# Two-layer transformer block on one Trainium2 core: the mixed stage's projections in three passes of fp32r parts

## The chip, the cores and the metric

The program runs on one core of a Trainium2 chip. The time is the device time of one execution in microseconds, here the median of 3 runs. TensorE multiplies, VectorE, ScalarE and GpSimd do the elementwise work, SyncE issues the DMAs that bring the weights. Each engine runs its own instructions in program order and waits on semaphores.

## The reference

Two blocks follow each other on 256 tokens of width 1024, each with two layers. The change is in the first block only. Per layer it computes, cut to what matters:

```
h = rms_norm(x, norm1_g[l]) * (1.0 + sc1) + sh1
proj = h @ w_in[l]                       # 1024 -> 5648 columns
da_q, da_k, da_v, dn_q, dn_k, dn_v, dn_z, dn_b, dn_a, gates = jnp.split(proj, ...)
y_a = diff_attention(da_q, da_k, da_v, lam, ...)          # 4 heads, rope, two softmaxes each
y_b = gated_deltanet(dn_q, dn_k, dn_v, dn_z, dn_b, dn_a, dn_conv[l], ...)  # conv, chunked scan
g_a, g_b = jnp.split(jax.nn.sigmoid(gates), 2, axis=-1)
merged = g_a * (y_a @ w_branch_a[l]) + g_b * (y_b @ w_branch_b[l])
x = x + gt1 * (merged @ w_out[l])
h = rms_norm(x, norm2_g[l]) * (1.0 + sc2) + sh2
x = x + gt2 * (jnp.square(jax.nn.relu(h @ w_mlp1[l])) @ w_mlp2[l])
```

All of it is float32. The second block (windowed and latent attention, 16 experts) is not touched.

## The kernel before

**Weights.** All weights of the first block pass through a ring of 5 slots in SBUF, 2 MB each (128 partitions x 4096 floats). A list, `order`, gives the sequence of the loads; each load waits until the last reader of the block that was in its slot is done. ada blocks are the weights of the modulation vectors (step r reads one each, `ada_row`), win blocks those of the projections, gate blocks those of z and the gates.

**Layer.** For each of the two layers: the norm and its transpose into hT (fp32, 8 chunks of 128 x 256); the dense stage lin3, which makes attention's q, k and v in 12 groups; the mixed stage; branch_b and merged_out; the MLP. lin3, the branch of attention, merged_out and the MLP multiply in three passes of fp32r: a number is cut into a high part (ScalarE casts it to fp32r) and a low part (VectorE subtracts the high part from the number), and the product is high x high, low x high and high x low. An fp32r matmul has one record in the trace, an fp32 matmul two.

**Mixed stage.** It interleaves attention, the short convolutions, the delta rule and the remaining projections. Its sequence is one table, `mix_order()` (line 169), that every engine walks; each engine has a function for the steps in which it takes part. The step f with n from 0 to 11 is one block of 128 columns of the delta rule's q, k and v, with n from 13 to 32 one of z and the gates: 8 fp32 matmuls that read the weights in the ring and hT, in two or four pieces (`f_parts`, line 206). f 33 to 36 are the branch of attention in three passes. f 12, 37 and 38 only free banks or read results. The other steps that the prediction speaks of:

- a_prep, a_scale, a_rope, a_sum, a_turn: attention's q and k get norm and rope, on VectorE, and are transposed. s_core, e_soft, m_top, k_comb, t_prob, c_prob, v_val, o_val: scores, softmax, combination, values. a_hn, d_hn: the norms of the heads.
- d_conv, d_silu, d_tok: the convolutions, their silu, and the transposes back. d_gate, d_gcum, d_l2, d_kqT, d_decay, d_LT: gates, cumulative sums and decays up to the triangular matrices.
- d_X, d_B, d_U: the triangular inverse by doubling, on TensorE in 64x64 matmuls, with VectorE and ScalarE taking turns. d_uw: u and w. d_S, d_gl, d_ws, d_out: the scan over four chunks in two directions.
- r: one block of a modulation's weights. b_hi, b_lo: the parts of the branch's weights.
- rates (line 775): the 32 small matmuls for beta and the decay, between lin3 and the mixed stage.

Of the kernel before, what the change touches and what calls it, by code (L numbers as in the profile page):

```python
# [10 lines left out]
ALU = mybir.AluOpType  # L11
# [157 lines left out]
def mix_order():  # L169
# [3 lines left out]
        ("f", 0, 0), ("a_prep",), ("a_scale",), ("f", 0, 1), ("a_rope", 0), ("f", 1, 0), ("f", 1, 1), ("f", 2, 0),  # L173
        ("f", 2, 1), ("f", 3, 0), ("f", 3, 1), ("f", 4, 0), ("d_conv", 0), ("a_rope", 1), ("a_rope", 2),
        ("d_conv", 1), ("f", 4, 1), ("f", 5, 0), ("a_rope", 3), ("d_conv", 2), ("d_conv", 3), ("f", 5, 1),
        ("a_sum",), ("f", 6, 0), ("f", 6, 1), ("f", 7, 0), ("f", 7, 1), ("r", 0), ("a_turn", 0), ("a_turn", 2),
        ("a_turn", 1), ("a_turn", 3), ("d_silu", 0), ("s_core", 0), ("e_soft", 0, 0), ("e_soft", 0, 1), ("f", 8, 0),
        ("s_core", 1), ("m_top", 0, 0), ("d_tok", 0), ("e_soft", 1, 0), ("m_top", 0, 1), ("m_top", 1, 0),
        ("f", 8, 1), ("e_soft", 1, 1), ("m_top", 1, 1), ("d_conv", 4), ("f", 9, 0), ("r", 1), ("f", 9, 1),
        ("f", 10, 0), ("k_comb", 0), ("f", 10, 1), ("f", 11, 0), ("f", 11, 1), ("d_conv", 5), ("k_comb", 1),  # L180
        ("s_core", 2), ("f", 12, 0), ("e_soft", 2, 0), ("t_prob", 0), ("t_prob", 1), ("c_prob", 0), ("m_top", 2, 0),
        ("d_conv", 6), ("m_top", 2, 1), ("d_conv", 7), ("c_prob", 1), ("r", 2), ("e_soft", 2, 1), ("d_silu", 1),
# [10 lines left out]
        ("f", 27, 3), ("d_X",), ("d_B", 1), ("d_U", 1), ("d_B", 2), ("d_U", 2), ("d_B", 3), ("d_U", 3), ("d_B", 4),  # L193
        ("r", 7), ("d_U", 4), ("d_B", 5), ("r", 8), ("d_U", 5), ("d_uw", 0), ("d_uw", 1), ("d_S", 0, 0),
# [58 lines left out]
def program(nc, a, c1off, c2off, out):  # L253
    ctx = ExitStack()
    with ctx:
# [132 lines left out]
        for l in range(2):  # L388
            for i in range(4 if l == 0 else 0):
                ada(0, 0, i)  # L390
            for j in range(3):
                if l and j < 2:
                    for i in (2 * j, 2 * j + 1):
                        ada(1, 1, i)
                cols(("win", l, j), a["w_in"][l], 512 * j, 512)
            for step, *key in mix_order():
# [7 lines left out]
                if step == "f" and n == 13:  # L404
                    cols(("gate", l, 0), a["w_in"][l], 3072, 512)
# [2564 lines left out]
```

## Time and profile before

| what | us |
|---|---|
| median of 3 runs | 2265.42 (2264.52 to 2266.91) |
| the profiled execution's span, first to last instruction | 2264.9 |
| TensorE busy | 1930.7 (85%) |
| VectorE busy | 908.8 (40%) |
| ScalarE busy | 631.8 (28%) |
| DMA, over the span | 272 GB/s |

The profile is one execution. Its own time, start and end of the program included, is not listed apart; the runs' median lies 0.5 us over the span. The first block is the first half of the span: layer 0's mixed stage from 77.7 to 306.6 us, layer 1's from 585.5 to 815. Busy times of an engine are to be read against the stretch they stand in, and an idle engine matters only where another waits for it.

### The profile page before, as it was taken

How to read it: one execution, taken by the hardware profiler on the slowest of the kernel's cores; microseconds unless marked ns; L12 is line 12 of the kernel's file. 1: busy time of each engine (PE TensorE's matmuls, PEld its weight loads, DVE VectorE, ACT ScalarE, POOL GpSimd, SP SyncE). 2: the span in 40 equal slices, each digit the busy share in tenths (PEclk: the TensorE clock that was granted, in tenths of full speed). 3: DMA queues.
4: the chain of work that ended last, by engine and by line, in shares of the span. 5: the costliest groups of instructions: out<-in, count | busy, mean ns of one | idle time of the engine just before them, and what ended most of it. 6: DMA issues, size and time to landing. Idle time of an engine off the chain costs nothing.

```text
span 2264.9 us, 31221 instructions
## 1 busy us (share of the span) xinstructions
PE 1930.7 (85%) x12944; PEld 1292.3 (57%) x12944; DVE 908.8 (40%) x1518; ACT 631.8 (28%) x1090; POOL 43.2 (2%) x46
## 2 busy tenths in 40 slices
PE   6999999999999999999999766666798996666666
PEld 3878888987878889987755311211276552122111
DVE  2665575645665576645754100000058520000001
ACT  3243335544243235534451100000044310000001
POOL 0001000000001000000000000000000000000000
PEclk9999999999999999999999988888899998887878
DMA  9554248556523244554438999999972689999997
GB/s 337 227 192 187 77 184 299 187 186 237 208 75 150 85 177 151 185 189 113 175 141 330 429 426 426 428 427 427 425 236 112 273 337 427 428 426 426 428 427 307
DMA packets 117302, 617.50 MB, mean 273 GB/s; under 512 B 18304, under 2 KB 21290, under 8 KB 83370
## 3 DMA queue, kind: packets, MB, share of 16 engines
q1 hardware_dynamic: 116586, 613.85, 68.3%
q8 instruction: 103, 1.69, 0.3%
q10 hardware_dynamic: 576, 1.66, 0.2%
q14 instruction: 37, 0.30, 0.0%
HBM read 614.44 MB, written 1.05 MB: 272 GB/s over the span
## 4 chain that ended last, share of the span: by engine, by line
PE 60%; DMA 27%; DVE 7%; ACT 3%; issue 1%; SPq 0%; POOL 0%; DVEq 0%; ACTq 0%
PE pb L640 58%; DMA ring<-in_w_up_dram 17%; DMA ar<-in_w_up_dram 4%; DMA hT<-in_w_up_dram 4%; PE pb L643 3%; DVE ar L1574 2%; DVE ar L1566 2%; ACT ar L2339 1%; DMA ring<-in_w_down_dram 1%; DVE ar L1578 1%; DMA ring<-in_ada_w_dram 1%; ACT ar L2343 1%; DVE small L1582 1%; DVE ar L1570 0%; ACT hT L2339 0%
## 5 line engine op out<-in xcount | busy, mean ns | idle before, releaser
L640 PE MATMUL pb<-ar 64*64 64x64 f32 (+10 forms) x3760 | 465.2, 379 | 101.0 <-DMA hT<-in_w_up_dram 43.6
L640 PE MATMUL pb<-ring,ar 128*32 128x512 f32 (+1 forms) x2160 | 367.6, 715 | 171.0 <-DMA ring<-in_w_up_dram 126.8
L640 PEld LDWEIGHTS pb<-ar 64*64 64x64 f32 (+5 forms) x3760 | 225.9, 145 | 273.0 <-issue 245.7
L2343 ACT COPY ar<-pb 128x512 f32<-128x512 f32 (+2 forms) x195 | 112.8, 579 | 948.3 <-PE pb L640 877.2
L1578 DVE COPY ar<-pb 128x512 f32<-128x512 f32 (+5 forms) x98 | 58.7, 599 | 760.9 <-PE pb L640 748.5
L640 PEld LDWEIGHTS pb<-ring,ar 128*32 128x32 f32 (+1 forms) x2160 | 98.4, 130 | 378.0 <-issue 368.4
L640 PE MATMUL pb<-hT,ring 128*128 128x256 f32 x1024 | 235.3, 388 | 0.0
L640 PEld LDWEIGHTS pb<-hT,ring 128*128 128x128 f32 x1024 | 196.2, 195 | 29.9 <-issue 3.4
L1566 DVE TENSOR_TENSOR ws<-ring,ws 128x1024 fp32r<-128x1024 f32 x128 | 156.9, 1226 | 123.5 <-ACT ws L2343 122.1
L640 PE MATMUL pb<-hs,ws 128*128 128x256 f32 x1536 | 186.3, 283 | 4.9 <-ACT hs L2343 2.4
L640 PEld LDWEIGHTS pb<-hs,ws 128*128 128x128 f32 x1536 | 184.7, 192 | 7.0 <-issue 2.3
L640 PE MATMUL pb<-ws,h1s 128*128 128x512 f32 x768 | 175.8, 390 | 0.0
L2343 ACT CAST ws<-ring 128x1024 fp32r<-128x1024 f32 x128 | 134.2, 1048 | 127.5 <-PE pb L640 123.9
L640 PEld LDWEIGHTS pb<-ws,h1s 128*128 128x128 f32 x768 | 144.0, 188 | 30.8 <-issue 1.0
L640 PE MATMUL pb<-wp,hp 128*128 128x512 f32 (+1 forms) x672 | 150.7, 383 | 7.3 <-ACT wp L2343 3.4
L640 PEld LDWEIGHTS pb<-wp,hp 128*128 128x128 f32 x672 | 121.3, 189 | 35.6 <-issue 4.6
L643 PE MATMUL pb<-c,ar 128*128 128x128 f32 (+3 forms) x620 | 96.1, 291 | 29.6 <-DMA c<-in_c_dram 9.0
L643 PEld LDWEIGHTS pb<-c,ar 128*128 128x128 f32 (+3 forms) x620 | 74.2, 157 | 80.3 <-issue 41.7
L1566 DVE TENSOR_TENSOR wp<-ring,wp 128x1024 fp32r<-128x1024 f32 (+1 forms) x56 | 64.9, 1159 | 68.2 <-ACT wp L2343 65.9
L2343 ACT CAST wp<-ring 128x1024 fp32r<-128x1024 f32 (+1 forms) x56 | 55.7, 994 | 72.0 <-PE pb L640 67.3
L1574 DVE SCALAR_TENSOR_TENSOR ar<-ar,pb 128x256 f32<-128x256 f32 (+1 forms) x84 | 40.7, 484 | 50.9 <-ACT ar L2339 34.1
L640 PE MATMUL pb<-ring,hT 128*128 128x512 f32 x128 | 59.4, 610 | 0.0
(162 smaller groups left out, 1658.9 us busy)
## 6 DMA issues: line engine op xcount, KB each, us to landing
ring<-in_w_down_dram SPq DMA_DIRECT2D x48, 2048.0 KB, 28.3
ring<-in_w_gate_dram SPq DMA_DIRECT2D x42, 2048.0 KB, 28.7
ring<-in_w_up_dram SPq DMA_DIRECT2D x42, 2048.0 KB, 23.8
ring<-in_w_mlp_dram SPq DMA_DIRECT2D x32, 2048.0 KB, 7.9
ring<-in_w_in_dram SPq DMA_DIRECT2D x28, 2048.0 KB, 11.3
ring<-in_ada_w_dram SPq DMA_DIRECT2D x24, 2048.0 KB, 8.3
ar<-in_w_gate_dram SPq DMA_DIRECT2D x12, 2048.0 KB, 27.4
ar<-in_w_up_dram SPq DMA_DIRECT2D x12, 2048.0 KB, 23.4
```

Of the source, the lines that this page charges most:

```text
L640: return e.matmul(o, l, r, start=start, stop=stop)
L643: return e.transpose(o, i, ident[0:i.shape[0], 0:i.shape[0]])
L1566: return e.tensor_tensor(o, i0, i1, op)
L1574: return e.scalar_tensor_tensor(out=o, in0=i0, scalar=s, in1=i1, op0=op0, op1=op1)
L1578: return e.tensor_copy(o, i)
L1582: return e.tensor_reduce(o, i, AX.X, op)
L2339: return e.activation(o, i, fn, scale=scale, **kw)
L2343: return e.copy(o, i)
```

## The change

- Step f for n < 33 is now 24 fp32r matmuls instead of 8 fp32 ones: high weights x high h, high weights x low h, low weights x high h.
- A new step g n makes the parts of f n's weights: ScalarE casts 128x1024 numbers into one of two buffers (`fhi`, in the place of hT), VectorE subtracts and writes the low part over the weights in the ring. The cast for f n waits until the second f before it is done. g 0 and g 1 run at the end of lin3.
- The parts of h, which lin3 makes for itself anyway, go into a ring slot and stay there until f 32 is done; in that time 4 slots are left for weights.
- rates moves from behind lin3 into its groups 6 and 7, one half each, since hT is overwritten afterwards.
- In the diff, the first function g is VectorE's and the second ScalarE's.
- `mix_order()` is another sequence, with the g steps in it. r 7 and r 8 stand before d_X, the casts and subtractions of the branch's weights partly later.

```diff
     return (
-        ("f", 0, 0), ("a_prep",), ("a_scale",), ("f", 0, 1), ("a_rope", 0), ("f", 1, 0), ("f", 1, 1), ("f", 2, 0),
...
+        ("f", 0, 0), ("f", 0, 1), ("f", 1, 0), ("a_prep",), ("f", 1, 1), ("g", 2), ("a_scale",), ("a_rope", 0),
...
+        fhi = [v4(zone_r(o, 1024), 8) for o in (-2048, -1024)]
+        F_ALL = [n for n in range(33) if n != 12]
...
+                if j == 1 - l:
+                    order.append(("parts", l))
                 cols(("win", l, j), a["w_in"][l], 512 * j, 512)
...
+                if step == "f" and n == 29:
+                    order.append(("parts_end", l))
...
+        def h_parts(site, l):
+
+            if site == "b":
+                return hp
+            s = place["parts", l][0]
+            return [v4(ring_r[s][:, 2048 * i:2048 * i + 2048], 8) for i in range(2)]
...
             def f(l, n, part):
...
+                    if part == 0:
+                        e.wait_ge(*A("g_hi", l, n))
+                    hi, lo = fhi[F_ALL.index(n) % 2], W_low(name)[:, :, 128 * (f0 + half):128 * (f0 + half) + 128]
+                    h_hi, h_lo = h_parts("a", l)
+                    for q in (((0,), (1,), (2,), (3,)) if f_parts(n) == 4 else ((0, 1), (2, 3)))[part]:
+                        if q == 2:
+                            e.wait_ge(*V("g_lo", l, n))
+                        for c in range(4 * (q % 2), 4 * (q % 2) + 4) if q > 1 else range(8):
+                            m = mm(pb[:, 256 * half:256 * half + 256], lo[:, c, :] if q > 1 else hi[:, c, :],
+                                   (h_lo if q == 1 else h_hi)[:, c, :], q == 0 and c == 0, q == 3 and c == 7)
...
+                    if g in (6, 7):
+                        rates(l, g - 6)
                 ahead(l)(3)
-                rates(l)
...
+            def g(l, n):
+
+                name, at = f_name(l, n)
+                e.wait_ge(*A("g_hi", l, n))
+                tt(W_low(name)[:, :, at], W(name)[:, :, at], fhi[F_ALL.index(n) % 2], ALU.subtract).then_inc(*V.up("g_lo", l, n))
...
+            def g(l, n):
+
+                name, at = f_name(l, n)
+                k = F_ALL.index(n)
+                if at.start == 0:
+                    e.wait_ge(*landed(name))
+                if k == 0:
+                    e.wait_ge(*P("ba", l, 1))
+                if k > 1:
+                    e.wait_ge(*f_done(l, F_ALL[k - 2]))
+                copy(fhi[k % 2], W(name)[:, :, at]).then_inc(*A.up("g_hi", l, n))
```

VectorE in layer 0 before the change, behind the scaling of q and k (rope is `ar<-xn,ar`, a convolution `ar<-ar,par`, a read of TensorE's result `ar<-pb`):

```order
L1566 TENSOR_TENSOR ar<-xn,ar 128x8x32 [waits dve_step] x2
L1578 COPY ar<-pb 128x2x256 [waits dve_step,pe_dn]
L1574 SCALAR_TENSOR_TENSOR ar<-ar,par 128x256 [waits dve_dn,act_conv0]
L1574 SCALAR_TENSOR_TENSOR ar<-ar,par 128x256 [waits dve_step] x3
L1566 TENSOR_TENSOR ar<-xn,ar 128x512 [waits dve_conv]
L1566 TENSOR_TENSOR ar<-xn,ar 128x8x32 [waits dve_step] x2
```

The same place on VectorE in the changed kernel; `ring_r<-ring,r 128x8x128` is the subtraction of a step g:

```order
L1606 TENSOR_TENSOR ar<-xn,ar 128x8x32 [waits dve_step] x2
L1618 COPY ar<-pb 128x2x256 [waits dve_step,pe_dn]
L1606 TENSOR_TENSOR ring_r<-ring,r 128x8x128 [waits dve_dn,act_g_hi]
L1614 SCALAR_TENSOR_TENSOR ar<-ar,par 128x256 [waits dve_g_lo,act_conv0]
L1614 SCALAR_TENSOR_TENSOR ar<-ar,par 128x256 [waits dve_step] x3
L1614 SCALAR_TENSOR_TENSOR ar<-ar,par 128x256 [waits dve_conv,act_conv0]
L1614 SCALAR_TENSOR_TENSOR ar<-ar,par 128x256 [waits dve_step] x3
L1606 TENSOR_TENSOR ring_r<-ring,r 128x8x128 [waits dve_conv,act_g_hi]
L1606 TENSOR_TENSOR ring_r<-ring,r 128x8x128 [waits dve_g_lo,act_g_hi]
L1606 TENSOR_TENSOR ar<-xn,ar 128x512 [waits dve_g_lo]
```

Steps g 3, 4 and 5 have come between the rope and the convolutions, and nothing has left VectorE.

TensorE in layer 0 before, in the doubling steps d_B 4 and d_U 4 (`ring,cact` is step r 7):

```order
L640 MATMUL pb<-ar 64x64 [waits act_B,dve_X,pool_AT]
L640 MATMUL pb<-ar 64x64 x15
L640 MATMUL pb<-ar 64x64 [waits dve_X,pool_AT]
L640 MATMUL pb<-ar 64x64 x15
L640 MATMUL pb<-ring,cact 32x512 [waits dma_ring_0]
L640 MATMUL pb<-ring,cact 32x512 x7
L640 MATMUL pb<-ar 64x64 [waits dve_XT,act_B]
L640 MATMUL pb<-ar 64x64 x15
```

TensorE in the changed kernel, the end of f 26, r 8, and the first matmuls of d_X:

```order
L673 MATMUL pb<-ring_r,r 128x256 [waits act_g_hi]
L673 MATMUL pb<-ring_r,r 128x256 x15
L673 MATMUL pb<-ring_r 128x256 [waits dve_g_lo]
L673 MATMUL pb<-ring_r 128x256 x7
L673 MATMUL pb<-ring,cact 32x512 [waits dma_ring_1]
L673 MATMUL pb<-ring,cact 32x512 x7
L673 MATMUL pb<-c,ar 64x64 [waits act_kqT,dve_XT]
L673 MATMUL pb<-c,ar 64x64 x15
```

r 8 has moved ahead of the doubling steps, and r 7 with it, a few rows further up.

SyncE's loads at the end of layer 0's MLP before, where the four ada blocks and the first win block for layer 1 are fetched:

```order
L2917 DMA ring<-in_ada_w_dram 128x2x2048 [waits dve_cut] x2
L2917 DMA ring<-in_w_in_dram 128x8x512 [waits dve_cut]
L2917 DMA ring<-in_ada_w_dram 128x2x2048 [waits dve_cut] x2
L2917 DMA ring<-in_w_in_dram 128x8x512 [waits pe_ada_row] x2
L2917 DMA ring<-in_w_in_dram 128x8x512 [waits dve_w_lo]
```

And in the changed kernel:

```order
L2982 DMA ring<-in_ada_w_dram 128x2x2048 [waits dve_cut] x2
L2982 DMA ring<-in_w_in_dram 128x8x512 [waits dve_cut]
L2982 DMA ring<-in_ada_w_dram 128x2x2048 [waits dve_cut]
L2982 DMA ring<-in_ada_w_dram 128x2x2048 [waits pe_ada_row]
L2982 DMA ring<-in_w_in_dram 128x8x512 [waits pe_ada_row]
L2982 DMA ring<-in_w_in_dram 128x8x512 [waits dve_w_lo]
```

With one slot taken by the parts of h, the fourth ada block waits for TensorE's reading of the first.

## Rows read from the trace of the kernel before

**Rows 1.** The page: busy tenths of engines and DMA in 40 slices.

```profile
PE   6999999999999999999999766666798996666666
DVE  2665575645665576645754100000058520000001
DMA  9554248556523244554438999999972689999997
```

**Rows 2.** Stretches: busy us of each engine (instructions), clock, DMA share, GB/s.

```profile
77.70:213.20 135.50, 132.67 (x799) 107.20 (x799) 92.94 (x192) 47.04 (x99) 4.67 (x3) 0.99 0.47 177
213.20:256.70 43.50, 41.61 (x1138) 37.85 (x1137) 15.85 (x23) 16.78 (x34) 8.74 (x8) 1.00 0.11 42
256.70:306.60 49.90, 49.10 (x385) 43.45 (x386) 34.01 (x46) 8.28 (x10) 1.64 (x1) 1.00 0.44 170
586.00:719.80 133.80, 129.72 (x740) 109.68 (x740) 92.44 (x191) 46.29 (x97) 4.66 (x3) 0.96 0.34 124
```

**Rows 3.** TensorE in time: start, us, what, matmul records.

```profile
73.92 3.90 PE L640 MATMUL pb<-wba,hT 128*128 128x16 f32 x32
122.11 8.90 PE L640 MATMUL pb<-hT,ring 128*128 128x256 f32 x40
213.24 0.97 PE L640 MATMUL pb<-c,ar 64*64 64x64 f32 x26
235.81 1.92 PE L640 MATMUL pb<-ring,cact 128*32 128x512 f32 x16
721.70 1.50 PE L640 MATMUL pb<-c,ar 64*64 64x64 f32 x44
```

**Rows 4.** A stretch within the MLP's three-pass matmuls.

```profile
400.00:425.00 25.00, 25.00 (x211) 25.00 (x210) 16.51 (x19) 14.06 (x18) 0.00 (x0) 1.00 0.53 195
```

**Rows 5.** Groups of instructions: a low part, and the page's casts.

```profile
L1566 DVE TENSOR_TENSOR ring_r<-ring,r 128x1024 fp32r<-128x1024 f32 x24 | 29.4, 1225 | 2.5
L2343 ACT CAST ws<-ring 128x1024 fp32r<-128x1024 f32 x128 | 134.2, 1048 | 127.5 <-PE pb L640 123.9
```

**Rows 6.** VectorE's waits from 77.7 to 213.2: us in total, times, longest.

```profile
DVE ar L1574 <- ACT ar L2339: 12.3, 7, 4.0
...
DVE small L1574 <- ACT small L2339: 3.4, 1, 3.4
...
DVE small L1570 <- POOL small L2840: 1.8, 1, 1.8
...
DVE small L1582 <- DVE ar L1574: 0.5, 1, 0.5
```

**Rows 7.** VectorE in time, layer 0: behind the dense stage, and in the decays.

```profile
76.55 0.17 DVE L1578 COPY ba<-pb 128x16 f32<-128x16 f32 x1
...
197.96 0.69 DVE L1566 TENSOR_TENSOR ar<-ar,c 128x512 f32<-128x512 f32 x1 [0.70 <-ACT ar L2339]
```

**Rows 8.** TensorE in part C of layer 0: d_out's first, the last of f.

```profile
281.11 1.96 PE L640 MATMUL pb<-ar 64*64 64x128 f32 x32
...
288.90 5.45 PE L640 MATMUL pb<-hT,ring 128*128 128x256 f32 x24
```

**Rows 9.** The seam of the layers: SyncE's issues, TensorE, and a landing time.

```profile
521.87 11.25 SPq L2917 DMA_DIRECT2D ring<-in_ada_w_dram  x2
...
538.52 3.64 PE L640 MATMUL pb<-ring,cact 128*32 128x512 f32 x32
...
544.98 3.64 PE L640 MATMUL pb<-ring,cact 128*32 128x512 f32 x32
...
ring<-in_ada_w_dram SPq DMA_DIRECT2D x24, 2048.0 KB, 8.3
```

**Rows 10.** Layer 1, TensorE behind a wait, and a stretch with its granted clock.

```profile
673.45 1.06 PE L643 MATMUL pb<-c,ar 128*128 128x128 f32 x8 [2.05 <-DVE ar L1574]
674.35 10.49 PE L640 MATMUL pb<-hT,ring 128*128 128x256 f32 x40
...
675.50:677.00 1.50, 1.50 (x5) 1.23 (x4) 0.70 (x4) 0.61 (x3) 0.00 (x0) 0.50 0.00 0
```

More of the change, by code:

```diff
@@ L178, in mix_order @@
[L178 to L182, printed above, removed]
@@ L203, in mix_order @@
+        ("d_gl", 2, 1), ("d_S", 1, 0), ("d_gl", 2, 0), ("d_ws", 2, 0), ("g", 30), ("f", 29, 0), ("d_ws", 2, 1),
[6 rows of a table added]
     )
@@ L455, in program @@
         for name in order:
+            if name[0] == "parts":
+                place[name] = line.pop(0)
+                continue
+            if name[0] == "parts_end":
+                line.append((place["parts", name[1]][0], ("parts", name[1])))
+                let_go["parts", name[1]] = None
+                continue
             if name[0] == "router":
@@ L789, in f @@
                     u, half = divmod(m, 2)
-                    j, f0 = u // 2, 2 * (u % 2)
-                    name = ("win", l, 3 + j) if kind == "dn" else ("gate", l, j)
-                    w = W(name)
+                    f0 = 2 * (u % 2)
+                    name, _ = f_name(l, n)
                     if half == 0 and part == 0:
-                        if n == 0:
-                            for cp in range(4):
-                                e.wait_ge(*(A if cp % 2 else V)("hT", "n1", l, cp))
-                        if f0 == 0:
-                            e.wait_ge(*landed(name))
                         open_bank[0] = bank(kind, l, u)
                     k, pb = open_bank[0]
-                    nc_ = 8 // f_parts(n)
-                    for c in range(nc_ * part, nc_ * part + nc_):
-                        m = mm(pb[:, 256 * half:256 * half + 256], w[:, c, 128 * (f0 + half):128 * (f0 + half) + 128],
-                               hT3[:, c, :], c == 0, c == 7)
-                    if half == 1 and c == 7:
+                    if part == 0:
[8 more added lines that the diff above has]
+                                   (h_lo if q == 1 else h_hi)[:, c, :], q == 0 and c == 0, q == 3 and c == 7)
+                    if q == 3 and half == 0:
+                        m.then_inc(*P.up("f", l, n))
+                    if q == 3 and half == 1:
                         m.then_inc(*P.up(kind, l, u))
@@ L808, in f @@
                             let_go[name] = P, kind, (l, u)
+                        if n == 32:
+                            let_go["parts", l] = P, kind, (l, u)
                         if u:
@@ L2043, in block1 @@
                              lambda cp: hT_out("n1", l, cp, lambda c: sa1[:, c:c + 1], lambda c: modT[:, c:c + 1], lambda cc: hT3[:, cc, :]))
-                for g in range(12):
-                    group(g)
-                    if l and g == 5:
+                for n in range(12):
+                    group(n)
+                    if l and n == 5:
                         mod(1, 1)
+                for n in range(2):
+                    g(l, n)
                 e.wait_ge(*P("lin", "a", l, 11))
@@ L2672, in block1 @@
                     ada_row(1, 1, room1[1])
-                for g in range(12):
-                    group(g)
-                    if g % 4 == 3:
-                        out_by(g // 4)
+                for n in range(12):
+                    group(n)
+                    if n > 9:
+                        g(l, n - 10)
+                    if n % 4 == 3:
+                        out_by(n // 4)
                 ahead(l)(3)
@@ L2689, in block1 @@
                     o_high(l, c)
-                for g in range(3):
-                    cut(l, g)
+                for m in range(3):
+                    cut(l, m)
                 squares("out", l)
@@ L2885, in small_loads @@
                     e.dma_start(sink[l], a["swa_sink_2"][l].partition_broadcast(128)).then_inc(*D.up("rows"))
-            for i, name in enumerate(order):
+            for i, name in enumerate(n for n in order if n[0] not in ("parts", "parts_end")):
                 s, before = place[name]
@@ L2908, in sync @@
                 elif before is not None:
-                    by, what, key = let_go.get(before, (P, "par", ()))
+                    by, what, key = let_go.get(before) or (P, "par", ())
                     e.wait_ge(*by(what, *key))
```

72 lines of the change are left out of this document (41 added, 31 removed), and 26 rows, old and new, of the table k.

## The prediction

> **What bounds the kernel now.** The slices of the page come first [rows 1]: TensorE is at nine tenths through the first half of the span, which is the first block, and the DMA engines are full only in the second half. The first block runs two layers; the change is in the mixed stage of each. The reader is to see in the table of stretches [rows 2] that TensorE is busy 132.67 of 135.50 us in the first part of layer 0's mixed stage (attention, convolutions and 28 of the 32 projection blocks; "part A" from here), 41.61 of 43.50 in the second (the doubling steps of the triangular inverse, "part B"), and 49.10 of 49.90 in the third (the scan, "part C"). Layer 1 is the same. So TensorE sets the pace now. But VectorE is no idle helper: in part A it works 92.94 us in 192 instructions, while in part B it works only 15.85 of 43.50. That unevenness decides my forecast.
>
> **TensorE's gain.** A projection block (one n of step f) is 8 fp32 matmuls of 128x256. 20 of them took 8.90 us (the row says x40, as each fp32 matmul leaves two records) [rows 3], so 0.445 us each: 3.56 us for a block. The new block is 24 fp32r matmuls of the same size; the MLP's, also with a weight load before each, ran 211 in 25 us [rows 4], 0.1185 each: 2.84 us. The gain is 0.72 us for each of 64 blocks, 46 us, if TensorE is what ends every wait. It will not be.
>
> **VectorE's cost in part A.** Each block's weights need a cast on ScalarE (1.05 us by the MLP's casts of the same size [rows 5]) and a subtraction on VectorE; the nearest row is the subtraction for the branch weights, 128x1024 into the ring, 1.225 us [rows 5]. By the order of the changed kernel, g of n = 2 to 26 without 12, 24 of them, stand on VectorE ahead of step d_X, which closes part A; the first two are done in the stage before, under its matmuls, and n = 27 to 32 after. Nothing is taken from VectorE. So its sum for part A in layer 0 is: 92.9 busy as before + 24 x 1.225 = 29.4 + what lies between instructions. That last is (135.5 - 92.9 - 33.0 of waits, eleven groups from 12.3 down to 0.5 [rows 6], - 1.7 behind its last instruction) / 192 = 0.04 us each, so 216 x 0.04 = 8.6. Waits that lie within one step cannot be filled by any sequence: 3.4 for ScalarE's two table loads in the gates and 1.8 for GpSimd's root [rows 6], and 1.4 for the exponentials of the decays (two waits of 0.70, the first in [rows 7]), 6.6 in all. Of the other 26 I leave 3, since casts and subtractions now stand in them. ScalarE has room: 47.0 + 24 x 1.05 = 72 of some 140 us.
>
> Where it starts: rates (3.90 us on TensorE [rows 3]) move into the stage before, groups 6 and 7. TensorE does the same work, but that stage's last group, on which attention's q and k wait, ends 3.9 us later, at 77.8 instead of 73.9, and VectorE's small work for lambda and the first copy of rates' result (done at 76.7 [rows 7], so 2.8 us, formerly beside rates) starts only there. Sum: 77.8 + 2.8 + 92.9 + 29.4 + 8.6 + 6.6 + 3.0 = 221.1. d_X could begin a good microsecond before VectorE's last instruction, so at 220.1, against 213.24 now [rows 3]: part A is 6.9 us longer in layer 0, although one block (f 27) has left it. In layer 1 there is no lambda work (but 1.6 us until ScalarE's squares are there) and part A begins at 586.0: 586.0 + 1.6 + 92.4 + 29.4 + 8.6 + 6.6 + 3.0 - 1.0 = 726.6 against 721.70 [rows 2, 3]: 4.9 longer. TensorE's own work in part A is 132.7 - 28 x 3.56 + 27 x 2.84 + two ada_row steps of 1.92 = 113.5 us [rows 2, 3], so it is idle some 28 us there. Bounds: with no wait at all, not even the unavoidable ones, and all lambda waits gone, VectorE's sum is 9.6 smaller (in layer 0 another 0.8), which is 3.5 and 4.7 us less than now; with every old wait kept it is 23 larger.
>
> **Part B.** Two ada_row steps, r 7 and r 8, stood between the doubling steps and TensorE had no wait around them; each took 1.92 us [rows 3]. Now both stand in part A, where TensorE has time. Their loads have to be there, and r 7's is issued behind the load of gate block 3; by my reckoning both land some 10 us ahead. Part B gets 3.8 us shorter in each layer. g 27 lies in VectorE's gaps there (15.85 busy of 43.50). Bounds: 0 and -3.8.
>
> **Part C.** TensorE does six blocks of 2.84 instead of five of 3.56: 17.0 for 17.8. VectorE gets g 28 to 32, 5 x 1.27 = 6.3 on 34.01 busy of 49.90 [rows 2]. Two of these stand ahead of the scan's first new values, and the cast of g 29 cannot start before f 27 is done (two buffers for high parts): 256.7 + 1.9 for two d_S + 2.8 for f 27 + 0.6 for a transpose = 262.0, + 1.2 for the cast and 1.3 for the subtraction = 264.5. From there to the last new values VectorE has 18 instructions of 0.69, each with its gap 0.72, and 5 of 1.27 (g 30, g 31, the low part of y and two of the branch's four low parts): 19.3, so 283.8. The outputs of the scan (d_out) need these; TensorE begins them at 281.11 now [rows 8], so +2.7. Behind that, 25.5 us now to the part's end, TensorE has 28 matmuls of 0.1185 = 3.3 us instead of the 12 of 5.45 [rows 8]; -2.1. The head norm ends some 0.4 us behind f 33 to 35. Sum +1.0 per layer. The first cast of the branch's weights waits for a load that is issued only when f 28 is done, at 265.4, since a slot is gone; it should be there at 273.7, 2 us ahead of its subtraction. Bounds: -0.8 (TensorE's work alone) and +6.3 (all of VectorE's shows).
>
> **One slot less at the layers' seam.** The fourth ada block before layer 1 was issued at about 533 behind VectorE's last cuts; now it waits for the first ada_row step, which starts at 538.52 and reads until 540.3 [rows 9]. Such a block lands after 8.3 us, at 548.6; TensorE reads it at 546.8 now [rows 9]. +1.8 us; bounds 0 and +4. At layer 0's start the DMA is full anyway and the same bytes go in the same sequence: 0.
>
> **The clock.** In layer 1 a single wait of 2.05 us in part A was followed by a stretch at granted clock 0.50, that is 1.2 of 2.4 GHz, and 20 matmuls took 10.49 us instead of 8.90 [rows 3, 10]: 1.6 us for one drop. The new part A has some 28 us of waits. Most of what a drop costs is time that TensorE has there anyway, but f n must end before the cast of n + 2 begins, so some comes through: I take 1.0 us per layer, bounds 0 and 12. The Trainium skill (TensorE: Matmul & The Clock Gate, "What's actually happening") says that the slow clock is the default and that activity releases it; the trace agrees with that at the wait of 2.05 us, and the rule speaks against every change that makes TensorE wait, as this one does.
>
> **Sum**: part A 6.9 + 4.9, part B -3.8 - 3.8, part C 1.0 + 1.0, seam 1.8, clock 2.0: +10.0 us. The profiled execution's span is 2264.9; what lies around it is about 0.5, as the median of the runs is 2265.4. All that follows the first block starts when its x is ready and shifts with it. So 2274.9 + 0.5 = 2275.4 us.
>
> **Rivals.**
> A, faster: the new sequence hides VectorE's waits altogether, even those within a step. Place: part A; price: up to 9.6 us of its sum per layer; the kernel is faster once over 5 of them are gone in both layers and part C loses nothing. At its end part A gives -3.5 - 4.7, part B -7.6, part C -1.6, seam and clock nothing: -17.4, 2248; half of that is 2256.7. For it: 26 of VectorE's 33 us of waits are of the kind that a subtraction fills. Against: table loads and roots stay in every layer.
> B, it pays for itself: VectorE's waits go down to those within a step, part C breaks even, the seam's load is early: 3.9 + 1.9 - 7.6 + 1.0 for the clock = -0.8, 2264.6. For it: the cast of nearly every g is ready ahead of its place. Against: softmax and silu still pass between two engines.
> C, the slow clock: TensorE has 28 us to spare in part A, and a block at half speed costs 2.84 more; from 10 of the 27 blocks on it sets the pace again. With half of them, 38 us, part A is 10 us longer per layer: 2293. For it [rows 10], where one wait of 2 us was enough; against: a slow block fills the wait that would bring the next drop.
> D, TensorE keeps the pace in part A and the 46 us come: 2219. VectorE's sum alone speaks against it.
>
> **Chances.** Forecast (2269 to 2283) 0.45; A 0.2; B 0.15; C 0.18; D 0.02. Two tenths of a per cent, 4.5 us, is what a measurement of this kernel can tell from no change. Faster takes A and D and a little of B, 0.23; within it stand most of B and the forecast's edge, 0.17; slower 0.60. Range 2256 to 2291: it takes half of A, all of B and most of C.
>
> **What would show it.** Right: VectorE busy over 85% of part A, TensorE waiting there some 28 us, mostly for VectorE's ring_r; d_X near 220; part B at 39 to 40 us; a granted clock under 0.95 in part A; TensorE waiting for an ada block at the seam. Wrong: TensorE continuously busy in part A (then the blocks or the subtractions cost other than I took), part B unchanged, or part C grown by over 5 us.

## The result: 0.94% slower, on the side I took, but twice as far

| | median us | ratio to before, 95% |
|---|---|---|
| before | 2265.02 (4 runs) | |
| changed | 2285.01 (4 runs, 2283.10 to 2290.44) | 1.0094 (1.0079 to 1.0108) |

I had forecast 2275.4, that is +10.0. It became +20.0 by the medians (0.88% by themselves; the ratio on record is 1.0094). The range 2256 to 2291 holds it.

The page of the changed kernel, the slices that answer to [rows 1]:

```profile
PE   6888999999888999999999866676698996676666
DVE  2778585655678586655673200000047530000001
DMA  9455248454625154554518999999983689999997
```

VectorE's digits grow where part A lies, TensorE's fall there. The stretches of the changed kernel, parts A, B, C of layer 0 and then of layer 1 (columns as in [rows 2]):

```profile
77.50:224.86 147.36, 125.69 (x1024) 106.00 (x1022) 122.27 (x224) 76.22 (x128) 3.78 (x3) 0.95 0.49 183
224.86:265.80 40.94, 40.15 (x1104) 39.42 (x1104) 18.94 (x26) 16.94 (x34) 9.66 (x9) 0.92 0.02 4
265.80:316.89 51.09, 50.25 (x449) 46.59 (x449) 39.83 (x52) 13.84 (x15) 1.64 (x1) 1.00 0.53 206
598.46:744.33 145.87, 121.36 (x974) 108.96 (x972) 120.28 (x215) 75.19 (x125) 3.77 (x3) 0.94 0.35 127
744.33:783.49 39.16, 38.91 (x1105) 38.17 (x1105) 18.96 (x26) 16.95 (x34) 9.66 (x9) 0.96 0.01 3
783.49:835.11 51.62, 50.78 (x452) 46.98 (x451) 39.93 (x52) 13.84 (x15) 1.64 (x1) 1.00 0.54 204
```

VectorE works 122.27 of 147.36 us in part A (92.94 of 135.50 before), in 224 instructions for 192; the 24 subtractions are there at the length of [rows 5], and the other eight are small ones for lambda and for the results of rates, which were done ahead of part A before. The granted clock is 0.95 and 0.94 in the two parts A, and 0.92 in the first part B.

From here on a part is measured from what TensorE does: A from the end of the dense stage and rates to the start of d_X, B to the end of the doubling steps and of u and w, C to the start of branch_b. Each number is a difference of two times in the timeline of one profiled execution:

| | A, layer 0 / 1 | B | C |
|---|---|---|---|
| before | 135.4 / 135.9 | 43.5 / 41.6 | 49.9 / 51.8 |
| changed | 147.2 / 145.7 | 40.9 / 39.2 | 51.1 / 51.6 |
| change | +11.8 / +9.8 | -2.5 / -2.4 | +1.2 / -0.2 |
| forecast | +6.9 / +4.9, and the clock's 1.0 each | -3.8 / -3.8 | +1.0 / +1.0 |

With +1.8 at the seam and +0.5 elsewhere, mostly in layer 1's dense stage, that is +20.0, as much as branch_b of layer 1 starts later. By the end of the second block 2.4 of them are gone again (the spans differ by 17.6); where they go I have not followed. So the two traces differ by less than the medians do, and that the medians and branch_b both give 20.0 is chance.

How VectorE spends part A of layer 0, its waits (us in total, times, longest), which answer to [rows 6]:

```profile
DVE small L1614 <- ACT small L2388: 3.4, 1, 3.4
DVE ring_r L1606 <- ACT r L2392: 2.1, 4, 1.2
DVE small L1610 <- POOL small L2905: 1.8, 1, 1.8
DVE ar L1606 <- ACT ar L2388: 1.4, 2, 0.7
...
DVE gper L1610 <- ACT gper L2388: 0.9, 1, 0.9
```

The 12.3 us at the head of [rows 6], the convolutions' waits for ScalarE, are gone; ScalarE's two table loads (3.4) and GpSimd's root (1.8) stand as before. What TensorE waits for in the same part, 21.7 us in all (147.36 - 125.69); its three largest:

```profile
PE pb L673 <- DVE ring_r L1606: 11.2, 5, 3.7
PE pb L673 <- ACT ar L2392: 3.8, 2, 3.0
PE pb L673 <- DVE ar L1606: 3.7, 1, 3.7
```

The first is VectorE's subtractions, the third d_X's wait. TensorE at the end of part A (start, us, what, matmuls, the wait before it):

```profile
219.28 1.92 PE L673 MATMUL pb<-ring,cact 128*32 128x512 f32 x16
224.86 1.44 PE L673 MATMUL pb<-c,ar 64*64 64x64 f32 x32 [3.66 <-DVE ar L1606]
227.09 1.97 PE L673 MATMUL pb<-c,ar 64*64 64x64 f32 x32 [0.79 <-DVE ar L1606]
```

r 8 is done, d_X waits 3.66 us for VectorE's last products, and its second half 0.79. What that wait does to the clock (same columns as the stretches):

```profile
224.50:227.50 3.00, 1.86 (x40) 1.67 (x42) 2.46 (x3) 0.59 (x1) 1.26 (x1) 0.67 0.00 0
227.50:230.50 3.00, 3.00 (x62) 3.00 (x60) 0.00 (x0) 0.59 (x1) 0.00 (x0) 0.50 0.02 5
230.50:233.50 3.00, 3.00 (x80) 3.00 (x78) 0.04 (x1) 1.17 (x2) 2.03 (x2) 0.69 0.00 0
```

The doubling steps begin at 0.50, 1.2 of 2.4 GHz. This was not in my sum: there I had charged the clock to part A alone. In layer 1 d_X also waits 3.66 us, and the clock falls for a shorter time:

```profile
744.00:747.00 3.00, 2.42 (x40) 2.23 (x42) 2.43 (x3) 0.79 (x2) 1.22 (x1) 0.56 0.00 0
747.00:750.00 3.00, 3.00 (x96) 3.00 (x94) 0.00 (x0) 1.17 (x2) 0.73 (x1) 0.87 0.00 0
```

The kernel before loses time to the clock as well, and not only behind waits. At the start of its part A in layer 1, right behind rates, TensorE is busy without a gap and the clock is at half:

```profile
584.50:586.00 1.50, 1.50 (x13) 1.50 (x13) 0.14 (x1) 1.02 (x1) 0.00 (x0) 0.91 1.05 403
586.00:587.50 1.50, 1.50 (x5) 1.14 (x5) 1.15 (x7) 0.00 (x0) 0.00 (x0) 0.50 0.23 82
587.50:589.00 1.50, 1.50 (x5) 1.23 (x4) 1.33 (x4) 0.00 (x0) 0.00 (x0) 0.50 0.00 1
```

The seam, finally, answers to [rows 9]:

```profile
555.41 1.92 PE L673 MATMUL pb<-ring,cact 128*32 128x512 f32 x16
558.89 1.92 PE L673 MATMUL pb<-ring,cact 128*32 128x512 f32 x16 [1.55 <-DMA ring<-in_ada_w_dram]
```

### The profile page after: what moved, and what is told of

Read it like the earlier page. It is cut to its first block, busy times and chain, and to the rows that moved or that the text cites. A ratio compares the mean times of both kernels' runs of the same rounds, so it can differ in the third digit from the quotient of the medians.

```text
span 2282.5 us, 32515 instructions
## 1 busy us (share of the span) xinstructions
PE 1910.4 (84%) x13456; PEld 1291.5 (57%) x13456; DVE 987.7 (43%) x1582; ACT 699.1 (31%) x1154; POOL 43.2 (2%) x46
## 4 chain that ended last, share of the span: by engine, by line
PE 51%; DMA 27%; DVE 14%; ACT 5%; issue 2%; SPq 0%; POOL 0%; DVEq 0%; ACTq 0%
PE pb L673 49%; DMA ring<-in_w_up_dram 16%; DMA hT<-in_w_up_dram 4%; DMA ar<-in_w_up_dram 4%; DVE ar L1606 4%; DVE ar L1614 3%; DVE ring_r L1606 2%; ACT ar L2388 2%; PE pb L676 2%; DVE small L1622 1%; DMA ring<-in_w_down_dram 1%; DVE ar L1618 1%; DMA ring<-in_w_in_dram 1%; ACT ar L2392 1%; DVE ar L1610 1%
## 5 line engine op out<-in xcount | busy, mean ns | idle before, releaser
L2392 ACT CAST ws<-ring 128x1024 fp32r<-128x1024 f32 x128 | 134.2, 1048 | 127.6 <-PE pb L673 123.6
L673 PE MATMUL pb<-ring_r,r 128*128 128x256 f32 (+1 forms) x1088 | 162.3, 297 | 3.4 <-ACT r L2392 3.4
L673 PEld LDWEIGHTS pb<-ring_r,r 128*128 128x128 f32 x1088 | 143.9, 196 | 10.0 <-ACT r L2392 4.8
L2392 ACT CAST r<-ring 128x1024 fp32r<-128x1024 f32 x88 | 92.3, 1049 | 109.5 <-PE pb L673 94.3
L1606 DVE TENSOR_TENSOR ring_r<-ring,r 128x1024 fp32r<-128x1024 f32 x88 | 107.8, 1225 | 15.5 <-ACT r L2392 7.4
L673 PE MATMUL pb<-ring_r 128*128 128x256 f32 x512 | 78.5, 298 | 19.7 <-DVE ring_r L1606 19.7
L673 PE MATMUL pb<-wp,hp 128*128 128x512 f32 (+1 forms) x384 | 82.2, 371 | 3.6 <-DVE wp L1606 2.2
L673 PEld LDWEIGHTS pb<-ring_r 128*128 128x128 f32 x512 | 68.8, 199 | 27.5 <-DVE ring_r L1606 22.4
```

The costliest lines, as they stand in the source:

```text
L673: return e.matmul(o, l, r, start=start, stop=stop)
L1606: return e.tensor_tensor(o, i0, i1, op)
L2392: return e.copy(o, i)
```

## The experiments

Each was timed against runs of the kernel before on the same chip; a ratio is to before unless said otherwise. What one kernel is said to take less or more than another is the difference of their ratios times 2264; by the intervals of the ratios such a difference is known to some 5 us where four runs stand behind it, and to some 3 where eight or more do. Parts are read from one profiled execution of each kernel.

### Is VectorE the pace of part A?

**Subtractions of an eighth.**

```diff
-  tt(W_low(name)[:, :, at], W(name)[:, :, at], fhi[..], ALU.subtract)
+  tt(W_low(name)[:, 0:1, at], W(name)[:, 0:1, at], fhi[..][:, 0:1, :], ALU.subtract)
-  mm(.., lo[:, c, :] if q > 1 else hi[:, c, :], ..)
+  mm(.., lo[:, 0, :] if q > 1 else hi[:, c, :], ..)
```

> The changed kernel, but VectorE's subtraction of each step g covers one eighth (128x128) of the weights, and TensorE's third pass reads that eighth eight times, so its work stays the same (the product lacks the rest of the low parts). VectorE theory: it sets the pace of part A. 24 subtractions there get 1225 - 294 = 0.93 us shorter, 22.3 us a layer; VectorE's own sum falls from 149.3 to 127 us, which is also about TensorE's (125.7 busy, of it some 7 by the slow clock, and a few waits on softmax). So d_X of layer 0 goes from 224.9 to between 203 and 207, part C stays within 1 us, and the median falls by 36 to 44 us, to 2241 to 2249. Rival, TensorE or the casts: what ends TensorE's waits is the slow clock or ScalarE's casts; the subtractions lie beside them; d_X stays above 215 and the median above 2265.

2253.83 us, ratio 0.9965 (0.9953 to 0.9976), 29 us less than the changed kernel. Part A 133.3 and 129.4 us: 13.9 and 16.4 shorter, where 22.3 of work were taken away. That is less than the 36 to 44 us that I expected, and far from the rival's 2265.

```profile
78.04:211.36 133.32, 120.88 (x1023) 102.73 (x1021) 99.84 (x224) 75.88 (x128) 3.77 (x3) 0.97 0.54 201
```

So VectorE did set the pace, but no further than to 133 us: there TensorE is busy 120.88, not my 113.5 (at a granted clock of 0.97), and waits take the rest, 6.3 us of them still for subtractions. Even with the subtractions almost free, part A of layer 0 is 2 us shorter than before, not the 19 that 27 blocks at 0.72 us would give.

**Each subtraction doubled.**

```diff
+  if 2 <= n <= 26:
+      tt(W(name)[:, :, at], W(name)[:, :, at], W(name)[:, :, at], ALU.max)
   tt(W_low(name)[:, :, at], W(name)[:, :, at], fhi[..], ALU.subtract)
```

> The changed kernel with a second instruction of the same size (128x1024, the weights' maximum with themselves, which changes nothing) on VectorE ahead of each of the 24 subtractions of part A. VectorE theory: 24 x (1.225 + 0.03 for the gap to an instruction of its own engine) = 30.1 us longer per layer, +60 us, median 2341 to 2347. Rival, TensorE and the casts have a share in the pace: the first ten or so of the added microseconds of each layer vanish in waits, median 2325 or less.

2338.64 us, ratio 1.0327 (1.0311 to 1.0342): 53 us more than the changed kernel. Part A 173.9 and 172.8: 26.7 and 27.1 longer for 30.1 of added work. Nine tenths of what is added to VectorE is added to the kernel. The median lies 2 us under the range of "VectorE alone" and 14 over its rival's. This is nearer to "VectorE alone" than to its rival, and 3 us per layer do go into waits. Its trace also gives the price of a fulfilled wait. VectorE in that kernel, start, us, what:

```profile
101.18 1.23 DVE L1606 TENSOR_TENSOR ring<-ring 128x1024 f32<-128x1024 f32 x1
102.44 1.23 DVE L1606 TENSOR_TENSOR ring_r<-ring,r 128x1024 fp32r<-128x1024 f32 x1
103.77 1.23 DVE L1606 TENSOR_TENSOR ring<-ring 128x1024 f32<-128x1024 f32 x1
105.03 1.23 DVE L1606 TENSOR_TENSOR ring_r<-ring,r 128x1024 fp32r<-128x1024 f32 x1
```

Here the added instruction carries the wait for ScalarE's cast, and the subtraction behind it waits for its own engine alone. 102.44 - 101.18 - 1.23 = 0.03 us lie ahead of the subtraction, 103.77 - 102.44 - 1.23 = 0.10 ahead of the other, and no wait is recorded there. An instruction that also waits for another engine costs 0.07 us more, even when the other has long been done. It is so throughout the changed kernel's part A in layer 0, counting the spaces of at most 0.15 us: they are 0.035 us on average ahead of the 135 instructions that wait for VectorE alone and 0.108 ahead of the 75 that also wait for another engine or a load, 12.9 us in all. Before the change they were 0.035 ahead of 130 and 0.108 ahead of 40, 8.9 us in all.

**Seven reads moved to ScalarE** (the kernel also has the idle matmuls of the next section).

VectorE loses these two lines (the first stands for every second pair of blocks), and ScalarE gets them:

```diff
-  copy(cin[:, 4 * j:4 * j + 2, 2:258], v4(ps("dn", l, u)[:, :], 2)).then_inc(*V.up("dn", l, u))
-  copy(oA[:, :, h, :], v4(ps("val", l, h)[:, 0:256], 2)).then_inc(*V.up("oa", l, h))
```

> The kernel with 7 idle matmuls ahead of d_X, and seven of VectorE's reads of TensorE's results in part A (three of 128x512 for the convolutions, 0.69 us, and four of 128x256 for attention's values, 0.42) on ScalarE instead. VectorE theory with the full price of an instruction that waits for another engine (its length and 0.1): 3.75 + 0.7 = 4.5 us less per layer, 9 us less than that kernel's 2278, median 2267 to 2271. Rival, ScalarE's turns are on the path: it casts late and TensorE waits for it; less than 3 us come, median 2275 or more.

2272.41 us, 1.0035 (1.0023 to 1.0048), 7.7 us less than the kernel with idle matmuls alone; part A 3.8 and 6.3 shorter. I had expected 9 less and 2267 to 2271; the 3.75 us of VectorE's time and seven spaces of 0.1 that come off each part A lie between its 3.8 and 6.3.

### The sequence, the slot and the two steps

**The new sequence with fp32 blocks.** The edit is the table of the changed kernel without its g steps, in the kernel before, and the one wait that the branch weights' last cast needs in it:

```diff
-        ("f", 0, 0), ("a_prep",), ("a_scale",), ("f", 0, 1), ("a_rope", 0), ...
+        ("f", 0, 0), ("f", 0, 1), ("f", 1, 0), ("a_prep",), ("f", 1, 1), ("a_scale",), ...
+                    if f0 == 6:
+                        e.wait_ge(*P("ws", l, 3, 0))
```

> The kernel before (projections in fp32, rates behind lin3, five slots for weights) with the new sequence of steps, without the g steps. Theory: the sequence by itself costs nothing. Part A has one projection block less (3.56) and r 7, r 8 more (3.84), TensorE waits a few us as before: 136 us; part B -3.8, part C +3.6. Median 2261 to 2269. Rival: the sequence itself delays attention or the convolutions, and the missing 5 us a layer of my forecast are its doing: d_X of layer 0 beyond 217, median 2275 or more.

2267.92 us, 1.0013 (1.0003 to 1.0024): +3 us. Part A 138.5 and 133.6 us, B 40.1 and 39.6, C 54.4 and 54.8 (with f 27 in it). d_X of layer 0 starts at 215.4, not beyond 217. The sequence alone is not where the missing 10 us are.

**The kernel before with one slot kept empty.**

```diff
+                if j == 1 - l:
+                    order.append(("parts", l))
...
+                if step == "f" and n == 29:
+                    order.append(("parts_end", l))
```

> The kernel before, with one slot of the ring kept empty exactly where the changed kernel keeps the parts of h in it. Nothing else differs. Theory: the fourth ada block at the layers' seam comes late, 1.8 us (forecast) to 2.4 us (the step between the two traces), and nothing at layer 0: median 1.8 to 2.4 us above before. Rival: the missing slot also delays win and gate blocks in the mixed stage, 5 us or more; or it costs nothing, and the seam of the changed kernel has another cause.

2280.08 us, 1.0069 (1.0054 to 1.0084): +15.6 us. That is outside what either theory said in size; the rival was the nearer. The seam costs +1.2 us (11.26 from the first ada_row step to lin3, for 10.03 before and 11.81 in the changed kernel). The rest is in part C, 58.5 and 59.2 us, 8.6 and 7.4 more. Part A is 2.4 us longer in layer 0 and 4.2 shorter in layer 1, with the blocks unchanged; in layer 1 the granted clock is 1.00 and not 0.96 as in the trace of before:

```profile
597.13:728.83 131.70, 126.98 (x749) 107.41 (x749) 92.81 (x191) 46.27 (x97) 4.66 (x3) 1.00 0.35 130
```

So a part read from one trace can be off by that much. SyncE's issue of the branch of attention's weights, in the kernel before and then with the slot empty:

```profile
200.91 2.24 SPq L2917 DMA_DIRECT2D ring<-in_w_branch_a_dram  x1
```

```profile
272.72 0.37 SPq L2930 DMA_DIRECT2D ring<-in_w_branch_a_dram  x1
...
280.67 4.44 ACT L2356 CAST r<-ring 128x1024 fp32r<-128x1024 f32 x4 [20.76 <-DMA ring<-in_w_branch_a_dram]
...
288.87 3.68 PE L651 MATMUL pb<-ar 64*64 64x128 f32 x32 [5.84 <-DVE ar L1579]
```

The load goes out 72 us later; ScalarE stands 20.76 us at the first cast, and behind it VectorE's low parts and TensorE's outputs of the scan. The changed kernel issues that load at 273.43, as late, and its part C is only 1.2 us longer in layer 0 and no longer in layer 1; its sequence has those casts behind the first half of f 29. So the new table goes with the slot: without it the slot costs 15.6 us, with it the seam's 1.8. That the place of the casts alone does it is my reading; the new table with fp32 blocks and a slot less was not run. I had priced the slot at the seam and for the first cast only, and had not seen that the old sequence could not have lived with it.

**r 7 and r 8 ahead of d_X in the kernel before.**

```diff
-  ("f", 27, 3), ("d_X",), ... ("r", 7), ("d_U", 4), ("d_B", 5), ("r", 8), ("d_U", 5),
+  ("f", 27, 3), ("r", 7), ("r", 8), ("d_X",), ... ("d_U", 4), ("d_B", 5), ("d_U", 5),
```

> The kernel before with r 7 and r 8 ahead of d_X instead of between the doubling steps; nothing else differs. Theory: the 3.8 us that part B of the changed kernel loses are worth something only because TensorE waits for VectorE in part A there. In the kernel before TensorE is full in part A, so part B is 3.8 us shorter and part A 3.8 us longer: median within 2 us of before. Rival: part B's own turns between the engines cover the two steps there, so that moving them out gives nothing in B and costs 3.8 us per layer in A: 2271.

2261.16 us, 0.9993 (0.9983 to 1.0003). B 37.9 and 37.7, A 137.6 and 138.6. B gives up 5.6 and 3.9 us and A takes 2.2 and 2.7 back; the median is the same within its interval, as the theory had it. So moved work was no gain that could be measured where it did not land in a wait.

### The clock

**Idle matmuls ahead of d_X.**

```diff
+    ("d_X",): (7, 7),        # matmuls by the identity, 0.44 us each, result unused
```

> The changed kernel with 7 idle matmuls of 0.44 us on TensorE in front of d_X, in the 3.66 us in which it waits for VectorE's last products. Clock theory: part B is 2.5 us shorter than before instead of 3.8 because TensorE runs at half clock for some 6 us behind that wait; with the wait filled the clock stays at 1.0 from 221 to 232 and part B is 1.3 to 2 us shorter per layer: median 2281 to 2283. Rival: part B lost the 1.3 us by the two halves of d_X waiting for VectorE (0.79 us), and the slow clock lies beside VectorE's and ScalarE's turns; median 2284 to 2286.

2278.02 us, 1.0069 (1.0054 to 1.0084), 5.7 us less than the changed kernel. TensorE there, and part B of layer 0:

```profile
219.42 3.29 PE L674 MATMUL pb<-c 128*128 128x256 f32 x14
223.13 1.15 PE L674 MATMUL pb<-c,ar 64*64 64x64 f32 x32 [0.42 <-DVE ar L1607]
```

```profile
223.13:261.70 38.57, 37.49 (x1104) 36.81 (x1105) 18.92 (x26) 16.93 (x34) 9.63 (x9) 1.00 0.02 4
```

Part B of layer 0 is 2.4 us shorter, with clock 1.00 for 0.92; the second half of d_X still waits (1.08), so here it was the clock, not the halves. In layer 1, where the clock also goes from 0.96 to 1.00, B gives 0.1. Of the rest 2.3 and 0.2 us are in part A, ahead of the idle matmuls; the kernels do not differ there, the granted clock is 0.95 in layer 0 in both, and in this run VectorE waited 0.7 us for casts instead of 2.1 and not at all for the gates. So what the filled wait is shown to give back is 2.5 us; the other 2.5 in these two traces, and what else is in the medians' 5.7, differs from run to run with the place of the slow stretches.

**Idle matmuls in part A too.**

```diff
+    ("d_X",): (7, 7), ("f", 2, 1): (7, 3), ("f", 3, 1): (3, 6), ("f", 4, 1): (5, 2),
+    ("f", 17, 1): (5, 5), ("f", 13, 0): (0, 7),
-    ("t_prob", 0): (2, 4)
+    ("t_prob", 0): (7, 4)
```

> The changed kernel with idle matmuls of 0.44 us not only ahead of d_X (7) but also in the longest waits of part A (7 and 3 ahead of the third pass of f 2 in the two layers, 3 and 6 at f 3, 5 and 2 at f 4, 5 and 5 at f 17, 7 in layer 1 ahead of f 13, 5 more in layer 0 ahead of the first probabilities), so that TensorE's clock stays up. VectorE theory: in part A the slow clock costs next to nothing, since VectorE sets the pace; against the kernel with the filled d_X alone at most 2 us per layer come back: median 2274 to 2279. Rival C of the prediction, the slow clock sets the pace in stretches: part A is 4 us or more shorter per layer, median 2270 or less.

2277.58 us, 1.0070 (1.0054 to 1.0085): the same as with d_X's alone.

```profile
77.50:222.55 145.05, 135.08 (x1087) 114.92 (x1086) 122.18 (x224) 76.20 (x128) 3.78 (x3) 0.99 0.48 185
594.84:737.70 142.86, 128.68 (x1033) 113.97 (x1032) 120.23 (x215) 75.20 (x125) 3.77 (x3) 0.99 0.34 129
```

With the clock at 0.99, part A is 2.2 and 2.8 us shorter than in the profile of the changed kernel; against the kernel with the filled d_X it is 0 and 2.6. Rival C wanted 4 and more in each. In layer 0 the clock went from 0.95 to 0.99 against that kernel and gave nothing. So the slow clock does not set part A's pace, and VectorE keeps it. In all the two kernels with idle matmuls are 5.7 and 5.4 us under the changed one, each known to some 5 us. The idle matmuls take TensorE's time too; what they cost where TensorE has no wait was not measured apart.

### Relief for VectorE

**Seven subtractions on GpSimd.**

```diff
+  PG = (3, 6, 9, 15, 18, 21, 24)       # these g on GpSimd, VectorE skips them
+  e.tensor_tensor(W_low(name)[:, :, at], W(name)[:, :, at], fhi[..], ALU.subtract)
```

> The changed kernel with 7 of the 24 subtractions of part A (n = 3, 6, 9, 15, 18, 21, 24) on GpSimd instead of VectorE. VectorE theory, with a g at its full price of 1.225 and about 0.15 around it: part A 9.6 us shorter per layer (137.8), median 2264 to 2268, provided that GpSimd's subtraction takes under some 3 us and leaves VectorE alone. Rival, a shared resource: VectorE's instructions get longer while GpSimd works, or GpSimd's subtraction takes 5 us or more and TensorE waits for it: part A within 3 us of 147.4 or longer, median 2279 or more. No trace so far shows a tensor_tensor of this size on GpSimd.

2294.12 us, 1.0145 (1.0128 to 1.0162), 11.5 us more. GpSimd needs 2.4 us for one, and the row below it is VectorE's rope at the same time; behind them the same rope in the changed kernel:

```profile
103.94 2.40 POOL L2927 TENSOR_TENSOR ring_r<-ring,r 128x1024 fp32r<-128x1024 f32 x1 [16.94 <-ACT r L2395]
...
102.87 5.40 DVE L1607 TENSOR_TENSOR ar<-xn,ar 128x512 f32<-128x512 f32 x6
```

```profile
101.95 3.26 DVE L1606 TENSOR_TENSOR ar<-xn,ar 128x512 f32<-128x512 f32 x6
```

```profile
77.80:228.76 150.96, 125.62 (x1023) 106.36 (x1022) 123.89 (x217) 76.17 (x128) 20.72 (x10) 0.94 0.47 178
```

Even a tiny instruction is held. The first of GpSimd's subtractions runs from 84.64 to 86.99 us; VectorE in that time, where the same two take 0.40 us in the changed kernel:

```profile
85.20 2.05 DVE L1611 TENSOR_SCALAR small<-small 128x32 f32<-128x32 f32 x2
```

VectorE has 8.6 us less to do and is busy 123.89 us instead of 122.27: its instructions are stretched by 10.2 us during GpSimd's 16.9. The Trainium skill (SBUF — State Buffer, "Who interferes with whom") says that a VectorE instruction with two inputs in SBUF and a GpSimd instruction that reads SBUF take turns on a shared port, the later one waiting in full; the rope's 2.14 us against GpSimd's 2.40 agree with it. The two 128x32 ones have one input, so that sentence is not about them.

**A hybrid.** Blocks 0 to 11 stay fp32 on hT, 13 to 32 go in three passes; the high parts of 13 to 24 lie where the gates come later, so that hT lives until block 11. Idle matmuls ahead of d_X.

```diff
-        F_ALL = [n for n in range(33) if n != 12]
+        fhi_a = [v4(zone_r(o, 1024), 8) for o in (ZG + 2048, ZG + 3072)]
+        F_ALL = list(range(13, 33))          # the others: 8 fp32 matmuls, no g
```

> A hybrid: blocks 0 to 11 stay 8 fp32 matmuls on hT, blocks 13 to 32 go in three passes; the high parts of 13 to 24 lie in a free zone so that hT lives until block 11; 7 idle matmuls ahead of d_X. So VectorE has 14 subtractions in part A instead of 24: 10 x 1.38 = 13.8 us less, TensorE 12 blocks at 3.6 instead of 3.2 us, 5 us more. VectorE theory: both engines need some 131 to 134 us for part A, d_X of layer 0 at 208 to 212 against 213.2 in the kernel before and 224.9 in the changed one; parts B and C as in the kernel with idle matmuls, seam +2.4: median 2252 to 2260, so faster than both. Rival, the sequence was made for the other load: TensorE or ScalarE wait in new places, d_X beyond 216, median 2268 or more.

2260.40 us, 0.9986 (0.9976 to 0.9995). Part A 135.8 and 135.4, not 131 to 134; d_X of layer 0 at 212.5, not by 212. The seven idle matmuls stand ahead of d_X here too, but part B of layer 0 takes 40.1 us at a granted clock of 0.96, for 38.6 at 1.00 in the kernel where they were tried first: behind them d_X still waits 0.58 us and its second half 1.08, and from 215.5 to 218.5 us the clock is 0.50. They do not keep it up every time.

**The hybrid with the seven reads on ScalarE.** The edit is both diffs together.

> The hybrid (blocks 0 to 11 fp32, 13 to 32 in three passes, 7 idle matmuls ahead of d_X) with seven of VectorE's reads moved to ScalarE. If VectorE still sets the pace of part A there (135.8 and 135.4 us), its 4.5 us come off as they did in the changed kernel: median 2251 to 2254, 9 below the hybrid's 2260. If TensorE does, with twelve fp32 blocks again in front and waits of 8 us in all, 1 to 3 us: median 2256 to 2260. I take the middle: both share the pace, 2255.

2254.08 us, 0.9967 (0.9957 to 0.9978): 7.5 us faster than before, as fast as the kernel that leaves work out (0.9965).

```profile
77.59:211.76 134.17, 127.94 (x940) 105.91 (x939) 106.12 (x207) 68.95 (x125) 3.77 (x3) 0.99 0.52 199
```

Part A 134.2 and 131.6, part B 38.9 and 39.1. The moved reads give 1.6 and 3.8 us of 4.5 in part A, which fits a shared pace.

**The hybrid with other fp32 blocks.**

```diff
-        F_ALL = list(range(13, 33))
+        F_ALL = [9, 10, 11, 13, 14, 15, 16] + list(range(21, 33))
```

> The same with another choice of fp32 blocks: 0 to 8 and 17 to 20, so three passes for 9, 10, 11, 13 to 16 and 21 to 32; 13 subtractions in part A instead of 14. In the hybrid VectorE waits for TensorE's scores early on (5.7 us) and TensorE waits for subtractions 18 to 20 later (1.5 and 2.5 us, and 2.9 for a cast). If two engines take turns as the bound, moving the fp32 blocks to where VectorE is late gives 2 to 4 us per layer over the hybrid with moved reads: median 2247 to 2252. If only the sum of VectorE's work counts, 1.4 us per layer: 2251 to 2254.

2257.85 us, 0.9983 (0.9975 to 0.9992), 3.6 us more than the last one (known to some 3), against both theories. Part A 135.7 and 133.2. So neither "put the fp32 blocks where VectorE is late" nor "only the sum counts" predicts this balance; why it lost is open.

## Why the prediction was off by ten

**The direction and the mechanism were right.** VectorE sets the pace of part A (both slopes, 0.6 to 0.7 downwards and 0.9 upwards), it is busy 83% there (I had said over 85%), TensorE waits mostly for its subtractions and d_X, though 21.7 us and not 28. Of the part's length, busy time was right: 124.4 us to VectorE's last instruction, of them 2.1 for lambda and rates, so 122.3 for my 92.9 + 29.4.

**Failed step 1: the spaces between VectorE's instructions.** I took "(135.5 - 92.9 - 33.0 of waits - 1.7) / 192 = 0.04 us each, so 216 x 0.04 = 8.6". In the changed kernel's layer 0, from 77.70 to VectorE's last instruction at 227.0, it is 149.3 - 124.4 busy - 12.1 of waits = 12.8 us, 0.057 for each of 225. An instruction that waits for another engine has 0.10 ahead of it, not 0.03. I took the average of the old mixture, in which 40 of 170 short spaces were of the long kind; in the changed kernel 75 of 210 are, since each g adds one, and where an old wait is gone its space of 0.10 stays, which I had counted into the 33 us of waits. So the term is 4.2 us too small, of which 24 x 0.07 = 1.7 are the subtractions' own.

**Step 2, the waits, was right apart from the clock.** With the clock kept up VectorE's waits were 9.5 us (without lambda's 0.9), forecast 6.6 + 3.0 = 9.6. In the changed kernel they were 11.8 on the same count: 1.3 more for casts and 0.9 for the gates. That slow blocks made these late is my reading; the kernel with the filled d_X has the same clock in part A and waits less. VectorE's last instruction so came 5.9 us later than I said; d_X began 2.2 us ahead of its end instead of 1.0.

**Failed step 3: the clock, "I take 1.0 us per layer".** With idle matmuls the kernel is 5.7 and 5.4 us shorter by the medians, 4.6 and 7.3 by the start of branch_b in the traces, so it is nearer 3 than 1 per layer, known to some 5 us in all. Of these, 2.4 us are tied to their place by an experiment: they lie where I had not looked, in part B of layer 0, behind the wait of 3.66 us that I had myself put ahead of d_X when I let TensorE be idle for 28 us. The same wait in layer 1 cost 0.1. I had also looked for drops behind waits alone, though the trace of before has one without a wait, behind rates.

**Added up**: in the kernel with idle matmuls in part A too, branch_b of layer 1 starts 12.7 us later than before, where my sum without the clock has 8.0. Part A is 9.6 and 7.0 us over before (forecast 6.9 and 4.9) and part B 4.9 and 3.0 under it (3.8 and 3.8). So part A's 4.8 us, which are the spaces in the main, are about half of the missing ten, and the clock with the waits that shift beside it, 7.3 in these two traces instead of 2, is the other half. These are single traces: layer 1's part A of before, from which I subtract, itself took 4.2 us more than in the trace of the empty slot. The seam came as forecast, 1.8. That "all that follows the first block ... shifts with it" was wrong by 2.4 us, in the forecast's favour.

**TensorE's share was too rosy but hidden.** I had 2.84 us for a block by the MLP's uninterrupted rows and 113.5 us for part A. With VectorE relieved it was busy 120.9, part of that by a clock of 0.97. Its blocks come in pieces between other shapes: in part C, 281.60 to 282.65 for eight matmuls that take 0.95 in a row. That did not show in the result, but it is one reason why the gain could not be had by relieving VectorE either.

**Rivals.** A fell (no old wait within a step went). B fell with part A, +11.8 and +9.8 for its 3.9 and 1.9, and with the seam. C is right that the clock costs more than I took, but not that it sets the pace. D fell at once.

**Range.** It held. The likeliest case's own 2269 to 2283 did not. It was kept wide upwards for rival C, the clock alone; about half of what the result lies above the forecast is the spaces, which had no bound of their own. So that it held is in part luck.

## What to carry to other kernels

Before moving work from a busy engine to an idle one, add up the idle one's instructions with the space before each, and take that space from instructions that wait for other engines, since a vanished wait leaves it. Where the sum says that TensorE will wait, look for the slow clock in what comes behind each long wait as well, not only in the stretch that holds it: behind a wait of 3.66 us it cost 2.4 us in one layer, which seven idle matmuls gave back, and 0.1 in the other. And a buffer taken from a ring of loads is priced by the latest load that it moves: list the issue times of all loads behind it, not only the next one's.

## What the hardware showed that I had not expected

- GpSimd's 128x1024 subtraction, 2.4 us, stops VectorE for most of that time (10.2 of 16.9 us in part A of layer 0), even at a tiny instruction: two 128x32 ones took 2.05 us instead of 0.40.
- A fulfilled wait for another engine costs VectorE 0.07 us (a space of 0.108 us for 0.035).
- Part B ran at a granted clock of 0.50 to 0.69 for some 6 us behind one wait of 3.66, and at 1.00 when that wait was filled with matmuls whose result nobody reads. The same filling in the first hybrid left it at 0.96.
- In the kernel before the clock stood at 0.50 from 586.0 to 589.0 us while TensorE was busy without a gap, behind the 128x16 matmuls of rates.
